# Mixture-of-experts stage: plain fp32 products in 64-token tiles with two column halves, instead of split products in 128-token tiles

## The chip, the cores and the metric

The kernel runs on one core of a Trainium2 chip. The time is the device time of one execution in microseconds; the profile shows one further execution. TensorE (PE) does matrix products, with its weight loads shown apart (PEld), VectorE (DVE), ScalarE (ACT) and GpSimd (POOL) do the rest, and SyncE (SP) issues most of the DMA transfers. Register, branch and semaphore instructions of an engine's sequencer carry a q behind the engine's name (PEldq for TensorE's).

## What is computed

One layer of a decoder trunk for 1024 prompt tokens and 32 sample tokens, in fp32: an adaLN modulation from a conditioning vector, a mixing sub-layer (differential attention beside a short gated convolution), then a channel sub-layer, and a last norm. The change concerns the channel sub-layer, a hierarchical mixture of 32 experts (4 groups of 8); each token goes to the best group and to two experts in it:

```
grp_prob = softmax(t @ w_rg + b_rg);  g_p, g_idx = top_k(grp_prob, 1)
in_grp   = (t @ w_re + b_re) of that group;  e_val, e_idx = top_k(in_grp, 2)
combine  = one_hot(g_idx * 8 + e_idx) weighted with softmax(e_val) * g_p
for e in range(32):
    hid = silu(t @ w_gate[e]) * (t @ w_up[e])          # 1024 -> 256
    out = out + combine[:, e:e+1] * (hid @ w_down[e])  # 256 -> 1024
```

There are 1056 tokens and so 2112 rows of work, and each expert has 3 MB of weights, 96 MB in all.

## The kernel before

Each engine has its own program, written out by hand; semaphores alone order them. In order of time come the modulation (w_ada, three-pass products), the projection to q, k, v (L584, plain fp32), the convolution branch (L612, plain fp32), attention over the prompt (L618 to L676), attention of the samples over the paged cache (L511 to L520 and L679 to L720, with four column groups of 32 addressed at once in L518 and L693), the output projection (three passes), and the expert stage with what plans it.

The plan. VectorE computes the two experts of each token (L1386 to L1414), counts rows per expert with a product (L776 to L778), gives each expert as many tiles of 128 rows as it needs and at least one (L1432 to L1434), sums them up, and writes `plan`: the expert of each tile, the running count of tiles per expert (from `INC`), and `MID`, from which the loops take their number. 18 pairs of selection matrices (L1469 to L1474) and as many products (L783) then give, for each tile and row, the token that is gathered (`xrow`) and the row that is written (`yidx`).

The steps. `expert_steps` (L320) runs the same pattern on every engine: two steps written out, a hardware loop over pairs of tiles, two steps at the end. Step j has buffer b = j % 2:

- TensorE (`expert_products`, L810) looks up the expert of tile j (`expert_of`, a register load from `plan`), finds its weight slot among two by two tests (`in_slot`, L339), and does gate and up at once, 512 columns in 8 chunks. `three_passes` (L526) does each chunk three times in fp32r: leading part by leading part, leading by rest, rest by leading. Then come the 8 transposes of tile j + 1 (L792), the down product of tile j - 1 in 2 chunks and 2 halves of 512 columns, again with a lookup and a search for the slot (`down_products`, L795), and two transposes of `hid` (L826).
- ScalarE (`expert_copies`, L1064) makes the leading part of new weights (L1037 and L1041, only when the expert changes), tanh of the gate (L1069), the leading part of the rows (L1056), the copy of y out of PSUM (L1062) and the leading part of hid (L1081).
- VectorE (`expert_rests`, L1499) makes all rests (L1488, L1492, L1496, L1517) and gated and hid (L1505, L1507).
- GpSimd (`move_rows`, L1649) copies the tile's index column and gathers tile j + 2 from `h2_dram` once tile j has been transposed, then scatters the y of tile j - 1 to `y_dram`.
- SyncE (`load_expert`, L461) loads gate and up of expert e + 1 when expert e - 1 has been multiplied, and down of expert e when down of e - 2 is done: two slots.

Behind the stage each token's two y rows are loaded (L489), weighted, gated, added and normalised.

Of the kernel before, what the change touches and what calls it, by code (L numbers as in the profile page):

```python
# [19 lines left out]
P = 128  # L20
# [14 lines left out]
MAXT = 2 * TOK // P + NE  # L35
# [13 lines left out]
for _name, _w in (("ident", P), ("mask", P), ("upper", P), ("iota", P), ("rope", NT * 96),  # L49
                  ("tokid", 2 * NT), ("valid", NT), ("dmask", LNEW), ("pair", 16), ("sub0", 1), ("sub1", 1),  # L50
                  ("half", 1), ("tilecol", 1)):
    _C[_name] = (_n, _n + _w)
    _n += _w
# [3 lines left out]
def constants():  # L57
# [11 lines left out]
    put("iota", np.broadcast_to(i[None, :], (P, P)).astype(np.float32))  # L69
    pos = np.zeros((NT, P), np.float32)  # L70
# [25 lines left out]
def build(nc, consts, x_prompt, x_sample, cache_k, cache_v, state_conv, page_table, c_prompt, c_sample,  # L96
# [19 lines left out]
    gate_v = w_gate[0].rearrange("e (p c) n -> e p c n", c=DC)  # L116
    up_v = w_up[0].rearrange("e (p c) n -> e p c n", c=DC)
    down_v = w_down[0].rearrange("e (p c) n -> e p c n", c=FC)

    with ExitStack() as ctx:  # L120
# [13 lines left out]
        O_AB, O_X, O_W, O_H, O_VKQ, O_MA = 8 * K, 24 * K, 60 * K, 108 * K, 141 * K, 189 * K  # L134
        cst = at("cst", 0, [P, NCONST])
        small = at("small", NCONST * 4 + 32 - (NCONST * 4) % 32, [P, 224])
        kTs = at("kTs", 6 * K + 960, [P, HEADS, NSAMP])
        qTs = at("qTs", 7 * K + 448, [P, HEADS, NSAMP])
# [83 lines left out]
        hsel = [at(f"hsel{i}", O_MA + 6 * K + 256 * i, [P, TCOLS]) for i in range(4)]  # L222
        xrow = at("xrow", O_MA, [P, TCOLS], I32)
        yidx = at("yidx", O_MA + 256, [P, TCOLS], I32)
# [5 lines left out]
        wgu = [at(f"wgu{i}", O_W + 16 * K * i, [P, 2, DC, FE]) for i in range(2)]  # L230
        wdn = [at(f"wdn{i}", O_W + 32 * K + 8 * K * i, [P, FC, D]) for i in range(2)]
        wguL = [at(f"wguL{i}", O_W + 16 * K * i, [P, 2, DC, FE]) for i in range(2)]
        wdnL = [at(f"wdnL{i}", O_W + 32 * K + 8 * K * i, [P, FC, D]) for i in range(2)]
        wguH = [at(f"wguH{i}", O_VKQ + 16 * K * i, [P, 2, DC, FE]) for i in range(2)]
        wdnH = [at(f"wdnH{i}", O_VKQ + 32 * K + 8 * K * i, [P, FC, D]) for i in range(2)]
        gidx = [at(f"gidx{i}", O_MA + 1024 + 32 * i, [P, 1], I32) for i in range(2)]
        sidx = [at(f"sidx{i}", O_MA + 1088 + 32 * i, [P, 1], I32) for i in range(2)]
        xg = [at(f"xg{i}", O_H + 24 * K + 4 * K * i, [P, D]) for i in range(2)]
        xgH = [at(f"xgH{i}", O_H + 4 * K * i, [P, DC, P]) for i in range(2)]
        xgL = [at(f"xgL{i}", O_H + 8 * K + 4 * K * i, [P, DC, P]) for i in range(2)]  # L240
        th = [at(f"th{i}", O_H + 16 * K + K * i, [P, FE]) for i in range(2)]
        hid = [at(f"hid{i}", O_H + 18 * K + K * i, [P, FE]) for i in range(2)]
        hidH = [at(f"hidH{i}", O_H + 20 * K + K * i, [P, FC, P]) for i in range(2)]
        hidL = [at(f"hidL{i}", O_H + 22 * K + K * i, [P, FC, P]) for i in range(2)]
        gated = [at(f"gated{i}", O_MA + 2 * K + K * i, [P, FE]) for i in range(2)]
        yrow = [at("yrow0", O_MA + 4 * K, [P, D]), at("yrow1", O_MA + 12 * K, [P, D])]
# [31 lines left out]
        ones = at("ones", O_H + 15 * K, [P, P])  # L278
        slot_i = at("slot_i", O_H + 14 * K + 256, [P, 2 * NT], I32)
# [13 lines left out]
        wgate_in0 wgate_in1 wup_in0 wup_in1 wdn_in0 wdn_in1 wguH_done wguL_done wdnH_done wdnL_done gidx_done sidx_done xg_in0 xg_in1 go_on  # L293
        xgT_ps xgH_done xgL_done gu_ps th_done hid_done hidT_ps hidH_done hidL_done y_ps y_done y_out0 y_out1
# [1402 lines left out]
```

## Time and profile before

| | |
|---|---|
| median of 3 runs | 1499.11 us (1498.01 to 1502.76) |
| the profiled execution | 1495.69 us, span 1493.8 us |
| TensorE products | 1235.5 us busy, 83% of the span |
| weight loads of TensorE | 846.9 us, 57% |
| VectorE | 745.9 us, 50% |
| ScalarE | 569.4 us, 38% |
| GpSimd | 264.0 us, 18% |
| HBM | 170 GB/s over the span |

Busy time is that of the engine's own instructions; products overlap their predecessors, so a busy TensorE is not one at its peak. The expert stage runs from about 984 us, the first gather, to about 1433 us, the last store of rows.

### The profile page before, as it was taken

Reading aid. Unit: us, or ns where it says so; the run is one execution under the profiler, and the core shown is the slowest. Engines: PE = TensorE matmul, PEld = TensorE weight load, DVE = VectorE, ACT = ScalarE, POOL = GpSimd, SP = SyncE. Lnnn points to the kernel's source line nnn. Section 1 sums busy time; section 2 is a strip of 40 time slices with the busy share of each in tenths; the row PEclk is TensorE's granted clock in tenths of the full one; section 3 lists DMA queues with packets and bytes.
Section 4 is the critical chain, followed back from the end, with each engine's and each line's share of the span. In section 5 each row is a group of like instructions: output and inputs, shape, how many; then the busy total and the mean of one; then the engine's idle time right before and its main releaser. Section 6 shows DMA issues by size and latency. Waiting matters only on the chain.

```text
span 1493.8 us, 20962 instructions
## 1 busy us (share of the span) xinstructions
PE 1235.5 (83%) x6201; PEld 846.9 (57%) x6202; DVE 745.9 (50%) x1101; ACT 569.4 (38%) x786; POOL 264.0 (18%) x289
## 2 busy tenths in 40 slices
PE   4879999999999689965787999458899999989920
PEld 1334444456666456644566787247777777777710
DVE  4772232101110787721113454658855656888747
ACT  4541110000000455542334222117744646777623
POOL 0020100010000111000000011013524334544323
PEclk9989999999999899986866999659999999999965
DMA  8991200011100200037777211408856667887545
GB/s 282 375 328 46 88 21 22 29 47 43 43 0 0 86 0 1 0 104 249 228 225 249 82 43 43 176 26 318 314 223 243 244 235 270 314 325 299 207 171 181
DMA packets 84547, 230.91 MB, mean 155 GB/s; under 512 B 16101, under 2 KB 28517, under 8 KB 72165
## 3 DMA queue, kind: packets, MB, share of 16 engines
q1 hardware_dynamic: 70288, 203.80, 38.5%
q0 software_dynamic: 14192, 26.24, 4.9%
q8 instruction: 39, 0.64, 0.2%
q14 instruction: 28, 0.23, 0.0%
HBM read 220.42 MB, written 34.21 MB: 170 GB/s over the span
## 4 chain that ended last, share of the span: by engine, by line
PE 57%; DVE 12%; issue 8%; SPq 7%; DMA 6%; ACT 5%; DVEq 2%; POOL 1%; ACTq 1%; POOLq 0%
PE psum L531 22%; PE psum L584 12%; PE psum L612 11%; SPq L407 3%; DMA xg<-h_scratch,gidx 2%; PE psum L630 2%; DVE xgL L1496 2%; DMA wada<-in_w_ada_dram 2%; DVEq L333 2%; PE psum L639 2%; SPq L416 1%; ACT pexp L925 1%; SPq L423 1%; PE psum L673 1%; PE psum L738 1%
## 5 line engine op out<-in xcount | busy, mean ns | idle before, releaser
L584 PE MATMUL psum<-wqkv,hT 128*128 128x512 f32 (+1 forms) x432 | 187.6, 594 | 0.0
L612 PE MATMUL psum<-hT,wcv 128*128 128x352 f32 x576 | 170.9, 459 | 0.0
L1488 DVE TENSOR_TENSOR wguL<-wgu,wguH 128x2048 fp32r<-128x2048 f32 x64 | 146.8, 2294 | 41.1 <-ACT wguH L1037 40.4
L531 PE MATMUL psum<-wguH,xgH 128*128 128x512 f32 x320 | 130.8, 409 | 32.8 <-DVE xgL L1496 32.8
L612 PEld LDWEIGHTS psum<-hT,wcv 128*128 128x128 f32 x576 | 109.3, 190 | 60.6
L584 PEld LDWEIGHTS psum<-wqkv,hT 128*128 128x128 f32 (+1 forms) x432 | 77.9, 182 | 103.2 <-issue 103.2
L1037 ACT CAST wguH<-wgu 128x2048 fp32r<-128x2048 f32 x64 | 120.2, 1910 | 20.4 <-issue 13.9
L531 PE MATMUL psum<-wguH,xgL 128*128 128x512 f32 x320 | 126.7, 396 | 0.0
L531 PE MATMUL psum<-wguL,xgH 128*128 128x512 f32 x320 | 126.4, 395 | 0.0
L1556 POOL TENSOR_SCALAR small<-small 128x1 f32<-128x1 f32 (+3 forms) x36 | 19.8, 551 | 467.5 <-ACT ajunk L1014 169.5
L630 PE MATMUL psum<-kT,qz 128*128 128x512 f32 (+3 forms) x192 | 77.7, 520 | 19.5 <-ACT pexp L925 18.2
L531 PEld LDWEIGHTS psum<-wguH,xgH 128*128 128x128 f32 x320 | 61.2, 191 | 50.2 <-issue 38.6
L1492 DVE TENSOR_TENSOR wdnL<-wdn,wdnH 128x2048 fp32r<-128x2048 f32 x32 | 73.2, 2288 | 14.8 <-ACT wdnH L1041 14.6
L1209 DVE TENSOR_TENSOR cuT<-psum,cg_sb 128x352 f32<-128x352 f32 (+1 forms) x12 | 6.2, 514 | 133.6 <-ACT cg_sb L911 133.5
L531 PE MATMUL psum<-wdnH,hidH 128*128 128x512 f32 x160 | 67.1, 420 | 5.1 <-issue 3.1
L1643 POOL COPY sidx<-yidx 128x1 int32 (+1 forms) x40 | 39.0, 975 | 182.4 <-ACT yrow L1062 182.3
L1041 ACT CAST wdnH<-wdn 128x2048 fp32r<-128x2048 f32 x32 | 61.0, 1906 | 26.3 <-issue 26.3
L531 PEld LDWEIGHTS psum<-wguH,xgL 128*128 128x128 f32 x320 | 61.1, 191 | 13.5
L531 PEld LDWEIGHTS psum<-wguL,xgH 128*128 128x128 f32 x320 | 61.3, 192 | 11.7
L911 ACT COPY cg_sb<-psum 128x352 f32<-128x352 f32 x12 | 5.4, 452 | 162.2 <-PE psum L612 162.2
L708 PE MATMUL psum<-cst,kseq 128*128 128x128 f32 x256 | 48.4, 327 | 22.6 <-DMA kseq<-in_cache_k_dram 21.9
L969 ACT COPY kTp<-psum 128x512 f32<-128x512 f32 x64 | 37.3, 586 | 76.6 <-PE psum L708 76.5
(269 smaller groups left out, 2320.7 us busy)
## 6 DMA issues: line engine op xcount, KB each, us to landing
wgu<-in_w_gate_dram SPq DMA_DIRECT2D x32, 1024.0 KB, 5.0
wgu<-in_w_up_dram SPq DMA_DIRECT2D x32, 1024.0 KB, 7.5
wdn<-in_w_down_dram SPq DMA_DIRECT2D x32, 1024.0 KB, 7.1
wada<-in_w_ada_dram SPq DMA_DIRECT2D x24, 1024.0 KB, 8.3
kseq<-in_cache_k_dram SPq DMA_DIRECT2D x64, 256.0 KB, 3.0
vseq<-in_cache_v_dram SPq DMA_DIRECT2D x64, 256.0 KB
yg<-y_scratch SPq DMA_DIRECT2D x16, 512.0 KB, 5.4
wqkv<-in_w_in_dram SPq DMA_DIRECT2D x1, 6144.0 KB, 24.9
```

The source lines that it names most:

```text
L407: return sp.value_load(pt_sb[0:1, s * PAGES + p:s * PAGES + p + 1], min_val=0, max_val=kc.shape[0] - 1)
L531: ins = mm(out, r32(x(c)), r32(w(c)), start=(begin and c == 0 and k == 0), stop=(end and c == chunks - 1 and k == 2))
L584: last = mm(psum[0:n, 2 + j, :], hT[:, c, P * t:P * t + n], wqkv[:, c, AW * j:AW * j + AW], start=(c == 0), stop=(c == DC - 1))
L612: last = mm(psum[:, 3 * (n % 2) + j, 0:TB], wcv[i % 2][:, c, j, :], hT[:, c, TB * tb:TB * tb + TB], start=(c == 0), stop=(c == DC - 1))
L630: last = mm(psum[:, 2 * u + a // 512, 0:b - a], qz[i % 2][:, u, h, :], kT[:, h, a:b], start=True, stop=True)
L708: last = tr(psum[:, 4 + n % 2, P * c:P * c + P], kseq[half % 3][:, p % 4, P * c:P * c + P], ident)
L969: nc.scalar.copy(kTp[n % 2][:, :, :], psum[:, 4 + n % 2, :].rearrange("p (c n) -> p c n", c=4)).then_inc(S["kp_sb"], 1)
L1037: nc.scalar.copy(r32(wguH[slot][:, g, :, :]), wgu[slot][:, g, :, :]).then_inc(S["wguH_done"], 1)
L1041: nc.scalar.copy(r32(wdnH[slot][:, :, :]), wdn[slot][:, :, :]).then_inc(S["wdnH_done"], 1)
L1488: TT(r32(wguL[slot][:, g, :, :]), wgu[slot][:, g, :, :], wguH[slot][:, g, :, :], ALU.subtract).then_inc(S["wguL_done"], 1)
L1492: TT(r32(wdnL[slot][:, :, :]), wdn[slot][:, :, :], wdnH[slot][:, :, :], ALU.subtract).then_inc(S["wdnL_done"], 1)
L1643: nc.gpsimd.tensor_copy(sidx[b][:, :], yidx[:, bass.ds(j, 1)]).then_inc(S["sidx_done"], 1)
```

## The change

Expert tiles hold 64 tokens. The row of a token is taken as two half rows of 512: a tile has 128 partitions, of which the first 64 hold the first halves of 64 tokens and the other 64 the second halves. Four transposes instead of eight turn them into `xT`, in which a chunk of 128 features has 64 token columns. All products are plain fp32 calls. Each chunk's 64 token columns are the stationary side of two calls that write PSUM partitions 0 to 63 and 64 to 127: for gate and up these are the two halves of the 256 hidden columns (128 of gate and 128 of up each), for down the two halves of the 1024 output columns. So gated, hid and y have 128 partitions and half the columns. The splits, their tiles and their semaphores are gone. Four slots hold whole experts; three experts are loaded as soon as the residual is done, the fourth once the router's inputs are free. The index columns are copied by VectorE instead of GpSimd. Four steps instead of two are written out ahead of the loop. The plan counts tiles of 64 by an addition and a shift instead of eight comparisons. The diff, cut to its core:

```diff
-MAXT = 2 * TOK // P + NE
+TW = 64
+NSLOT = 4
+MAXT = 2 * TOK // TW + NE
...
-    gate_v = w_gate[0].rearrange("e (p c) n -> e p c n", c=DC)
-    down_v = w_down[0].rearrange("e (p c) n -> e p c n", c=FC)
+    gate_v = w_gate[0].rearrange("e (h p k) n -> e p h k n", h=2, k=4)
+    down_v = w_down[0].rearrange("e (c p) n -> e p c n", c=FC)
+    h2_halves = h2_dram.rearrange("t (h c) -> (t h) c", h=2)
+    y_halves = y_dram.rearrange("r (h c) -> (r h) c", h=2)
...
+        LEAD = 4
         def expert_steps(eng, step, mid):
-            for b in range(2):
-                step(b, b, 0, True, 2)
+            for j in range(LEAD):
+                step(j, j % 2, j // 2, 2)
             with eng.Fori(0, mid) as m:
                 for b in range(2):
-                    step(2 * m + (2 + b), b, m + 1, False, 2)
+                    step(2 * m + (LEAD + b), b, m + LEAD // 2, 2)
...
-        def in_slot(eng, e, body, new=1):
-            for slot in range(2):
-                bit = (e + (1 - slot)) & 1
-                with eng.If(((bit + new) >> 1) > 0):
+        def in_slot(eng, e, body):
+            for slot in range(NSLOT):
+                with eng.If(((e + (NSLOT - slot)) & (NSLOT - 1)) < 1):
                     body(slot)
...   SyncE
             sp.wait_ge(W["x1_done"], 2 * NT)
-            load_gate_up(0, 0)
+            for e in range(3):
+                load_gate_up(e, e)
+                load_down(e, e)
...
+            sp.wait_ge(W["rexp_in"], 2)
+            sp.wait_ge(W["lg_ps"], NT)
+            load_gate_up(3, 3)
+            load_down(3, 3)
...
+            with sp.Fori(0, NE // NSLOT - 1) as m:
+                for slot in range(NSLOT):
+                    e = NSLOT * m + (NSLOT + slot)
+                    before = sp.value_load(plan[0:1, bass.ds(e + (INC - NSLOT), 1)], min_val=1, max_val=MAXT)
+                    sp.wait_ge(W["gu_ps"], before)
+                    load_gate_up(e, slot)
+                    sp.wait_ge(W["y_ps"], before)
+                    load_down(e, slot)
...   TensorE
             def gather_transposes(b):
-                for c in range(DC):
-                    last = tr(psum[:, c // 4, P * (c % 4):P * (c % 4) + P], xg[b][:, c:D:DC], ident)
+                for k in range(4):
+                    last = tr(psum[:, b, P * k:P * k + P], xg[b][:, k:512:4], ident)
...   down_products
-                    pe.wait_ge(W["hidL_done"], j + 1)
-                    pe.wait_ge(W["wdnL_done"], e + 1)
-                    for n in range(2):
-                        a = slice(512 * n, 512 * n + 512)
-                        last = three_passes(psum[:, 5 + n, :], lambda c: hidH[b][:, c, :], lambda c: hidL[b][:, c, :],
-                                            lambda c: wdnH[slot][:, c, a], lambda c: wdnL[slot][:, c, a], FC)
+                    pe.wait_ge(W["hidT_sb"], j + 1)
+                    pe.wait_ge(W[f"wdn_in{slot}"], 16 * (e >> 2) + 16)
+                    for c in range(FC):
+                        for n in range(2):
+                            last = mm(psum[TW * n:TW * n + TW, 5 + b, :], hidT[b][:, TW * c:TW * c + TW], wdn[slot][:, c, 512 * n:512 * n + 512],
+                                      start=(c == 0), stop=(c == FC - 1))
...   expert_products
-                    pe.wait_ge(W["xgL_done"], j + 1)
-                    pe.wait_ge(W["wguL_done"], 2 * e + 2)
-                    three_passes(...).then_inc(S["gu_ps"], 1)
+                    pe.wait_ge(W["xT_sb"], j + 1)
+                    pe.wait_ge(W[f"wgu_in{slot}"], 32 * (e >> 2) + 32)
+                    for c in range(DC):
+                        h, k = divmod(c, 4)
+                        for n in range(2):
+                            last = mm(psum[TW * n:TW * n + TW, 2 + b, 0:FE].rearrange("p (g f) -> p g f", g=2), xT[b][:, k, TW * h:TW * h + TW],
+                                      wgu[slot][:, :, h, k, P * n:P * n + P], start=(c == 0), stop=(c == DC - 1))
+                    last.then_inc(S["gu_ps"], 1)
...   VectorE, one step (expert_rests before)
+            def expert_rows(j, b, i, left):
                 dve.wait_ge(W["th_done"], j + 1)
+                STT(gated[b][:, :], th[b][:, :], 1.0, psum[:, 2 + b, 0:P], ALU.add, ALU.mult).then_inc(S["m_dve_step"], 1)
                 dve.wait_ge(S["m_dve_step"], j + 1)
+                STT(hid[b][:, :], gated[b][:, :], 0.5, psum[:, 2 + b, P:2 * P], ALU.mult, ALU.mult).then_inc(S["hid_done"], 1)
+                if left == 2:
+                    dve.wait_ge(W["xgT_ps"], j + 1)
+                    gather_index(j + 2, b)
+                if past(j, 1):
+                    scatter_index(j - 1, 1 - b, i - 1 + b)
+                dve.wait_ge(W["hidT_ps"], j + 1)
+                nc.vector.tensor_copy(hidT[b][:, :], psum[:, 4, 0:P]).then_inc(S["hidT_sb"], 1)
...   GpSimd, one step
                 if left == 2:
-                    pool.wait_ge(W["xgT_ps"], j + 1)
-                    pool.sem_inc(S["go_on"], 1)
                     gather_rows(j + 2, b)
-                if not (first and b == 0):
+                if past(j, 1):
                     scatter_rows(j - 1, 1 - b)
```

`past(j, n)` is true in the loop and for written-out steps from n on. In a step ScalarE keeps tanh (128 columns), the copy of the transposed rows (512) and the copy of y (512). `expert_rests` and `expert_copies` lose the rest.

## Rows read from the trace of the kernel before

**Rows 1.** Page, part 4: the chain that ended last, share of the span by line.
```profile
PE psum L531 22%; PE psum L584 12%; PE psum L612 11%; SPq L407 3%; DMA xg<-h_scratch,gidx 2%; PE psum L630 2%; DVE xgL L1496 2%; DMA wada<-in_w_ada_dram 2%; DVEq L333 2%; PE psum L639 2%; SPq L416 1%; ACT pexp L925 1%; SPq L423 1%; PE psum L673 1%; PE psum L738 1%
```

**Rows 2.** Windows: stretch, its length, engines' busy us (instructions), clock, DMA share, GB/s.
```profile
997.20:1101.60 104.40, 91.58 (x405) 74.52 (x406) 80.09 (x62) 72.53 (x62) 38.23 (x31) 0.94 0.75 286
1101.60:1250.50 148.90, 138.44 (x656) 114.21 (x655) 82.92 (x80) 78.24 (x79) 55.89 (x60) 0.99 0.59 223
1250.50:1418.00 167.50, 153.16 (x735) 126.75 (x734) 139.35 (x109) 126.09 (x109) 74.98 (x60) 1.00 0.77 293
```

**Rows 3.** Line L1069: duration ns min/median/max, first and last start.
```profile
L1069 ACT ACTIVATE th<-psum x40: 370/385/385, 1005.8 to 1421.4; 128x256 f32<-128x256 f32 x40
```

**Rows 4.** Chain of waits of one step: start us, us, what.
```profile
1247.42 5.75 PE psum L531 x24
...
1253.61 0.43 DVE gated L1505
...
1256.68 1.23 DVE xgL L1496
```

**Rows 5.** Timeline, TensorE, plain fp32: start us, us, instruction, count.
```profile
326.89 15.36 PE L612 MATMUL psum<-hT,wcv 128*128 128x352 f32 x51
...
667.21 0.43 PE L518 MATMUL psum<-kTp,qbd 128*32 128x128 f32 x8
...
722.42 3.64 PE L693 MATMUL psum<-vseq,aTs 128*32 128x128 f32 x64 [0.54 <-DVE aTs L1308]
```

**Rows 6.** Chain of waits near 1412: transposes, then a down product.
```profile
1411.97 0.88 PE psum L792 x8
1412.85 2.77 PE psum L531 x12
```

**Rows 7.** TensorE's sequencer: a read and tests, 1243.9:1245.3; 1255.7:1256.8; all tests.
```profile
L333 PEldq FUSED_REGOPS  x2: 43/100/157, 1244.0 to 1244.5; - x2
...
L343 PEldq ALU_OP  x2: 32/34/36, 1244.8 to 1244.8; - x2
...
L813 PEldq ALU_OP  x1: 36/36/36, 1245.2 to 1245.2; - x1
...
L343 PEldq ALU_OP  x3: 36/36/36, 1255.7 to 1256.3; - x3
...
L343 PEldq COMPARE_BRANCH  x160: 67/154/357, 993.9 to 1424.2; - x160
```

**Rows 8.** TensorE's sequencer: two waits that it reached, by line.
```profile
L609 PEldq EVENT_SEMAPHORE  x1: 51/51/51, 335.9 to 335.9; - x1
...
L706 PEldq EVENT_SEMAPHORE  x1: 51/51/51, 725.0 to 725.0; - x1
```

**Rows 9.** A full gather; landings of L1637 in 1262:1400, 1120:1165 and 990:1010.
```profile
1250.41 3.01 POOL L1637 DMA_INDIRECT xg<-h_scratch,gidx  x1 [0.86 <-POOL gidx L1634]
...
DMA to landing us min/median/max: 7.7/8.2/8.9
...
DMA to landing us min/median/max: 5.2/7.9/10.5
...
DMA to landing us min/median/max: 3.0/4.6/9.2
```

**Rows 10.** DMA queues, 1262:1400: packets, MB, share of 16 engines.
```profile
q1 hardware_dynamic: 5643, 41.07, 76.4%
q0 software_dynamic: 3744, 2.67, 6.0%
```

**Rows 11.** DMA queue of code, 1000:1400: blocks, MB, share.
```profile
q8 instruction: 2, 0.03, 0.0%
```

**Rows 12.** First transposes; end of the stage (timeline, then chain of waits).
```profile
992.75 1.97 PE L792 MATMUL psum<-cst,xg 128*128 128x128 f32 x8 [11.02 <-DMA xg<-h_scratch,gidx]
...
1429.06 1.02 ACT yrow L1062
...
1433.90 4.77 DMA yg<-y_scratch
```

More of the change, by code:

```diff
@@ L227, in build @@
         vmap = at("vmap", O_MA + 8 * K, [P, 3, TCOLS])
[L230 to L235, printed above, removed]
+        SLOT = (O_W, O_W + 24 * K, O_VKQ, O_VKQ + 24 * K)
+        wgu = [at(f"wgu{i}", SLOT[i], [P, 2, 2, 4, FE]) for i in range(NSLOT)]
+        wdn = [at(f"wdn{i}", SLOT[i] + 16 * K, [P, FC, D]) for i in range(NSLOT)]
         gidx = [at(f"gidx{i}", O_MA + 1024 + 32 * i, [P, 1], I32) for i in range(2)]
         sidx = [at(f"sidx{i}", O_MA + 1088 + 32 * i, [P, 1], I32) for i in range(2)]
[L238 to L246, printed above, removed]
+        xg = [at(f"xg{i}", O_H + (16 + 2 * i) * K, [P, 512]) for i in range(2)]
+        xT = [at(f"xT{i}", O_H + (20 + 2 * i) * K, [P, 4, P]) for i in range(2)]
+        yrow = [at(f"yrow{i}", O_H + (24 + 2 * i) * K, [P, 512]) for i in range(2)]
+        th = [at(f"th{i}", O_H + 28 * K + 512 * i, [P, P]) for i in range(2)]
+        gated = [at(f"gated{i}", O_H + 29 * K + 512 * i, [P, P]) for i in range(2)]
+        hid = [at(f"hid{i}", O_H + 30 * K + 512 * i, [P, P]) for i in range(2)]
+        hidT = [at(f"hidT{i}", O_H + 31 * K + 512 * i, [P, P]) for i in range(2)]
         gate_fp = at("gate_fp", O_AB, [P, D]); gate_fs = at("gate_fs", O_AB + 4 * K, [P, D])
@@ L1078, in expert_copies @@
-                if not (first and b == 0):
-                    copy_y(j - 1, 1 - b, i - 1 + b, not first)
-                act.wait_ge(W["hidT_ps"], j + 1)
-                nc.scalar.copy(r32(hidH[b][:, :, :]), psum[:, 4, 0:FE].rearrange("p (c n) -> p c n", c=FC)).then_inc(S["hidH_done"], 1)
+                    copy_rows(1 - b)
+                if past(j, 1):
+                    copy_y(j - 1, 1 - b, i - 1 + b)
             act.wait_ge(W["xgT_ps"], 1)
-            lead_rows(0)
+            copy_rows(0)
@@ L1479, in _ @@
             link(TT(vmap[:, 1, :], vmap[:, 1, :], vmap[:, 0, :], ALU.add))
+            for k in range(2):
+                link(TS(vmap[:, k, :], vmap[:, k, :], 2.0, C("side"), ALU.mult, ALU.add))
             link(nc.vector.tensor_copy(xrow[:, :], vmap[:, 1, :]))
             nc.vector.tensor_copy(yidx[:, :], vmap[:, 0, :]).then_inc(S["plan_done"], 1)
-            mid = dve.value_load(plan[0:1, MID:MID + 1], min_val=NE // 2 - 2, max_val=MAXT // 2 - 2)
-            def rest_gate_up(e, slot, g):
-                dve.wait_ge(W["wguH_done"], 2 * e + (g + 1))
-                TT(r32(wguL[slot][:, g, :, :]), wgu[slot][:, g, :, :], wguH[slot][:, g, :, :], ALU.subtract).then_inc(S["wguL_done"], 1)
@@ L1511, in expert_rests @@
-                if first and b == 0:
-                    rest_down(0, 0)
-                else:
-                    e = expert_of(dve, j)
-                    in_slot(dve, e, lambda slot: rest_down(e, slot), step_of(e, expert_of(dve, j - 1)))
-                dve.wait_ge(W["hidH_done"], j + 1)
-                TT(r32(hidL[b][:, :, :]), psum[:, 4, 0:FE].rearrange("p (c n) -> p c n", c=FC), hidH[b][:, :, :],
-                   ALU.subtract).then_inc(S["hidL_done"], 1)
-            for g in range(2):
-                rest_gate_up(0, 0, g)
```

177 lines of the change are left out of this document (70 added, 107 removed).

## The prediction

> **What bounds the kernel now.** I read the chain of waits first. A fifth of the span is TensorE in L531, the three-pass product, and most of that lies in the expert stage, the only stage that this change rewrites [rows 1]. The table by stretch says that this stage is not TensorE alone: over its three thirds the engine counts 92, 138 and 153 us of 104, 149 and 168, the clock is nearly always the full 2.4 GHz, and the DMA engines move 223 to 293 GB/s [rows 2]. So neither is full. The gate/up product of the first tile ends at 1005.8 (where its tanh starts) and that of the fortieth at 1421.4 [rows 3]: 39 steps of 10.66 us, 415.6 us. The chain of one step tells what a step is: 5.75 us of products, then gated and hid, then VectorE's remainders of weights and rows up to the end of xgL at 1257.9, and only then the next product [rows 4]. The split's remainders on VectorE hold each step, not the products.
>
> **The change part by part.**
>
> *Number of steps.* The reference's routing on its own inputs gives, per expert, 67 65 7 28 28 50 9 10 | 87 286 176 142 110 120 229 354 | 27 11 12 17 34 48 48 7 4 28 6 16 52 5 20 9 rows. In tiles of 128, with at least one each, that is 39, padded to 40; in tiles of 64 it is 53, padded to 54. So 39 steps become 53. Twenty-two of the 53 are experts with one tile.
>
> *What goes.* All splits and remainders (wguH, wguL, wdnH, wdnL, xgH, xgL, hidH, hidL): the chain of rows 4 loses its VectorE part, and ScalarE and VectorE keep half-width work of some 2 us a step each. What is late next has to be found among the array, TensorE's sequencer, the gathers and the loads.
>
> *The array.* A plain fp32 call runs as two events with two weight loads (288 calls of L612 are 576 events). In the convolution 51 of them take 15.36 us, of which the last one lasts 0.46: 0.298 us for 352 columns, 0.847 ns a column [rows 5]. Do two column halves run at once? In L518, where four groups of 32 columns are addressed, 8 events fit into 0.43 us though each lasts about 0.27, and in L693 64 start in 3.2 us, 0.051 each, where one event of 128 columns alone needs 0.108 at the full clock [rows 5]. They do. Gate/up is then 8 chunks x 2 x 256 columns = 3.47 us, down 2 x 2 x 512 = 1.73, four transposes half of today's 0.88 [rows 6], the hid transpose 0.11: 5.75 us; with up to 0.4 for four changes between tiled and whole array, 5.75 to 6.2. Today's is 5.75 + 0.88 + 2.77 + 0.23 [rows 4, 6].
>
> *TensorE's sequencer.* This is the term that I think decides. Each step looks for its slot twice (gate/up and down), now among four slots instead of two, and every test costs whether taken or not. Reading the expert number takes from 1244.0 to 1244.8, 0.76; a test that is entered from there to L813 at 1245.2, 0.45; one that is skipped 1255.7 to 1256.3, 0.6 [rows 7]. The new test has one register operation less (no shift), 0.12 by the spacing of the operations: 0.33 and 0.48. Two searches are 2 x (0.76 + 3 x 0.48 + 0.33) = 5.05 us; counters, waits with a register value and the loop 0.85 more (8 operations of about 0.1). Now 3.3 of this is hidden behind 10.66 us. Does it hide still? The sequencer runs ahead of the array by a bounded count: at 335.9 it reached the wait behind the second group of L612, which had begun at 326.9; 30 of 48 events had started, so 18 events and their loads, 36 instructions, were outstanding. At 725.0, in the tiled L693, some 22 events, 43 instructions [rows 5, 8]. I take 38. Gate/up is 64 instructions, at 0.054 us each; so 26 must be through before the sequencer leaves it: 1.4 us. Issuing the other 26 instructions 0.3. Sum: 5.05 + 0.85 + 1.4 + 0.3 = 7.6 us a step, above the array's 6.2. If the shift stays in the test, 8.6; if most of the search hides, the array's 6.2.
>
> *Gathers.* A gather's index is now copied on VectorE behind hid, so gather j+2 starts about 2.2 us after gate/up j ended (tanh, gated, hid at half width, the index, and the 0.86 in front of the DMA [rows 9]), and it has to be there before the transposes behind gate/up j+1. From those transposes to the end of the next gate/up are about 6.0 us. So two steps need 2.2 + L + 6.0, L being issue to landing. L is 8.2 us in the median while weights load, 7.9 where tiles are mixed, and 3.0 at the least; a full gather keeps POOL 3.0 us instead of 1.0 [rows 9]. With L = 8.2 a step is 8.2 us, with 4.5 it is 6.4. Today the weights' packets are 8 KB and the rows 4 KB; both halve, so I expect a shorter L; the gathers stay at or just under 7.6 and I add 0.3 for those that don't: **7.9 us a step**, the value nearest to both rows.
>
> *Weight loads.* In the single-tile stretch the weight queue holds the 16 engines 76.4% and the gathers and scatters 6.0% of steps of 10.6 us [rows 10]: 8.1 + 0.64 = 8.75 us of transfer an expert. Experts 16 to 31 are sixteen such steps, but three slots are full when expert 15 ends: 13 loads of 8.75 = 114 us against 15 steps of 7.9 = 118. Just hidden. If steps were 6.2 this would bind there, for some 20 us.
>
> *Ends.* The first transposes started at 992.75 at the half clock [rows 12]; four instead of eight, half a copy, no xgL, and 2 x 3.47 at the half clock put the first gate/up's end at 1001.4 instead of 1005.8; with the index copied on VectorE, -5 us. Behind the last gate/up lie 12.1 us until the rows are stored, before yg is loaded at 1433.9; without hidH, hidL and with half the copy of 1.02 [rows 12] about 10: -2. The plan drops eight 0.2 us comparisons for four operations and gains three: nothing. The 9 MB loaded ahead run while the plan is made; nothing on the path waits for that queue but the stores of h2, 0 to 2 us, within the range.
>
> **Sum**, against the profiled execution's own 1495.7 us (span 1493.8 and 1.9 around it): 1495.7 - 5 - 2 - 415.6 + 53 x 7.9 = 1491.8. The median shown is 3.4 above that execution, so 1495, against 1499.1. Each of 39 steps becomes 2.8 us shorter, 108 us, and 14 new ones of 7.9 come in, 111. Even is 8.0 us a step.
>
> **The rivals.**
>
> *A step is the array's (6.4 us).* For it: were the sequencer free to run further ahead, the 1.4 us of stall and much of the search would vanish behind the products. Against: rows 8. Time: 1073.1 + 53 x 6.4 = 1412, 1416 in the median. The Trainium skill (Advanced Engine Details and Errata, Engine Queue Depths) gives TensorE 64 places "complicated with tiling", which would let the whole of gate/up in at once. The trace shows 36 and 43.
>
> *The gathers set the step: the side on which it is slower.* Place: the transposes waiting for xg. It decides from L = 7.8 us on. With 8.4 for the 22 single tiles (8.3 a step) and 9.8 for the 31 full ones (9.0; their POOL time is the 3.0 us of rows 9, and loads of 3 MB run into them) it is 1073.1 + 183 + 279 = 1535, 1538 in the median. For it: today's 7.7 to 8.9 in a loaded queue. Against: the packets halve.
>
> *Code is fetched anew.* TensorE's loop grows from about 390 to about 780 instructions; today no more than 2 blocks of code came in 400 us [rows 11]. Were it three blocks per two steps at some 2 us each, a step would be 10.9 and the kernel 1654. The Trainium skill (Runtime: NRT & Kernel Launch, Instruction fetch mechanics) says that a taken branch out of the loaded window waits for a DMA of code, and gives TensorE room for 2048 instructions. By that figure the loop fits; no row of this trace shows that size.
>
> *The halves do not run side by side* (64 wide groups are not in this trace, 32 wide ones are): 5.2 us more in the array, 11.2 a step, 1670.
>
> **How the numbers follow.** Forecast with steps of 7.5 to 8.4, 1474 to 1522 around 1495: 0.58. Array's step 0.15, gathers 0.14, code 0.07, halves one after the other 0.06. Within 0.3% (about what a measurement of this kernel can tell from no change) means steps between 7.9 and 8.05: 0.11, all of it in the forecast, which gives 0.27 to faster and 0.20 to slower. With the rivals: faster 0.42, same 0.11, slower 0.47. The range, 1425 to 1555, holds the forecast, the gathers' case and more than half of the array's; it leaves out 0.13 for the last two and 0.06.
>
> **What would show it.** Steps from tanh to tanh of 7.5 to 8.4 us, 54 of them, with the register operations of L343 busy nearly throughout; L531 gone from the stage; pairs of fp32 events starting together; waits before the gate/up product put down to issue, not to xT or the weights. Wrong: steps at 6.2 to 6.5 (the search hides), waits on xg longer than 1 us in most steps, tanh waiting 10 us or more, a code queue that runs all through the stage, or weights late before the last expert.

## The result and the profile after

The changed kernel takes 1519.0 us in the median of four runs (1511.8 to 1521.2), the kernel before took 1499.0 us beside it: ratio 1.0128, interval 1.0101 to 1.0155. The forecast was 1495 us, no difference; it is 1.3% slower, inside the stated range, on the side that the forecast gave 0.47. The profiled execution has a span of 1517.9 us against 1493.8, and all of the 24.1 us is in the expert stage.

The tanh behind the gate/up products (line 1059 of the changed kernel), which answers to [rows 3]; columns: duration min/median/max, first and last start:

```profile
L1059 ACT ACTIVATE th<-psum x54: 277/277/278, 1001.7 to 1448.6; 128x128 f32<-128x128 f32 x54
```

There are 54 of them, so the tile count was right. Forty tiles took 415.6 us from first to last; 54 take 446.9, or **8.43 us for each of 53 steps**, where 7.9 was forecast and 8.0 was even. The start came 4.1 us earlier (1001.7 for 1005.8), the part behind the last tanh is 3.1 us shorter (69.3 us of span for 72.4). Together: -4.1 - 3.1 - 415.6 + 446.9 = +24.1.

The same stage by windows, answering to [rows 2] (stretch, length, busy us with instructions of TensorE products, weight loads, VectorE, ScalarE, GpSimd, then clock, DMA share, GB/s):

```profile
1001.72:1448.55 446.83, 357.98 (x2377) 185.91 (x2377) 56.84 (x263) 76.13 (x158) 105.89 (x104) 0.97 0.64 236
987.00:1100.00 113.00, 86.52 (x536) 44.35 (x536) 12.90 (x63) 17.12 (x36) 24.59 (x24) 0.88 0.69 253
1100.00:1300.00 200.00, 159.46 (x1086) 83.97 (x1088) 26.13 (x121) 34.99 (x73) 49.21 (x49) 0.99 0.46 163
1300.00:1455.00 155.00, 123.96 (x812) 63.25 (x808) 19.30 (x89) 26.05 (x54) 35.26 (x35) 0.96 0.75 286
```

VectorE and ScalarE have little left to do (57 and 76 us of 447). TensorE's products fill 358 of 447 us, so 89 us are idle. The clock is lower in the first and last stretch, where the DMA share is higher, than in the middle one; the first stretch also begins at the half clock.

Two pieces of the chain of waits show the two kinds of step. A quiet one, from 1101.37 to 1109.87 (start us, us, what):

```profile
1101.37 3.67 PE psum L822 x32
...
1105.07 0.75 PE psum L796 x4
1105.82 0.69 issue
1106.51 1.94 PE psum L808 x8
1108.44 0.26 PE psum L833
1108.70 1.17 issue
1109.87 3.67 PE psum L822 x32
```

Nothing is late here but TensorE's own sequencer: "issue" stands ahead of the down products (L808) and of the next gate/up (L822). The same trace shows how far the sequencer runs ahead, the 1.4 us in the prediction's sum. It reaches the wait in front of this gate/up (L818) at 1101.2 and the first instruction behind it, a test of the next search (L346), at 1102.7; TensorE's timeline up to 1102.73 stands below them:

```profile
L818 PEldq FUSED_REGOPS  x1: 75/75/75, 1101.2 to 1101.2; - x1
L346 PEldq ALU_OP  x1: 32/32/32, 1102.7 to 1102.7; - x1
1101.37 1.73 PE L822 MATMUL psum<-wgu,xT 128*64 128x256 f32 x14 [1.56 <-issue]
```

When it leaves the gate/up, 14 of its 32 events have started: 18 events with their weight loads, 36 instructions, are still out. For about 1.4 us in every step it can't search.

Now a step with a late gather, behind the tanh at 1370.94, and below it the window 1378 to 1390 (columns as above):

```profile
1372.80 5.82 DMA xg<-h_scratch,gidx
...
1378.66 0.75 PE psum L796 x4
1379.41 1.92 issue
1381.33 3.68 PE psum L808 x8
1385.01 0.41 PE psum L833
1385.42 4.30 PE psum L822 x32
...
1378.00:1390.00 12.00, 9.42 (x48) 4.38 (x49) 0.86 (x5) 1.40 (x3) 2.03 (x2) 0.72 0.91 351
```

The rows land at 1378.62. The down search, which follows the wait for them in TensorE's order, could not start before: 1.92 us of issue. Then the down products take 3.68 where the quiet step has 1.94, and the gate/up 4.30 for 3.67, at the lower clock level after the idle time: the granted clock was 0.72 from 1378 to 1390 and 1.00 in the 12 us before. The next gate/up ends at 1389.72, 11.1 us behind the landing. This is one of the dearest cases. In 13 steps the products of the transposes waited for rows; from the start of these transposes to the next tanh they took 8.2 to 11.4 us, 9.5 in the mean. Slow products are not in all of them: 6 of the 53 down products took over 3 us.

TensorE's waits between the first and the last tanh (engine, line, waited for: us, times, longest), and below them the test instructions, the landings of all 54 gathers, and the DMA queue of code in 1050 to 1440 (blocks, MB, share):

```profile
PE psum L822 <- issue: 47.5, 40, 2.1
PE psum L808 <- issue: 28.9, 27, 2.1
PEld psum L796 <- DMA xg<-h_scratch,gidx: 18.6, 18, 2.1
PE psum L796 <- DMA xg<-h_scratch,gidx: 10.5, 13, 1.6
```

```profile
L346 PEldq COMPARE_BRANCH  x424: 77/208/437, 1003.6 to 1448.5; - x142
...
DMA to landing us min/median/max: 2.1/4.9/7.2
...
q8 instruction: 1, 0.02, 0.0%
```

The 424 comparisons are 8 for each of 53 steps. Eighteen weight loads of transposes waited for rows, and in 13 of these cases the products too. By stretch the landing's median is 3.4 us in 1100 to 1300 and 5.8 in 1300 to 1440.

### The profile page after: what moved, and what is told of

It is laid out like the page before. It is cut to its first block, busy times and chain, and to the rows that moved or that the text cites. A ratio compares the mean times of both kernels' runs of the same rounds, so it can differ in the third digit from the quotient of the medians.

```text
span 1517.9 us, 20398 instructions
## 1 busy us (share of the span) xinstructions
PE 1211.3 (80%) x6791; PEld 714.2 (47%) x6792; DVE 493.1 (32%) x1112; ACT 362.6 (24%) x691; POOL 193.1 (13%) x237
## 4 chain that ended last, share of the span: by engine, by line
PE 60%; issue 10%; DMA 9%; DVE 8%; SPq 8%; ACT 3%; POOL 1%; POOLq 0%; DVEq 0%; ACTq 0%
PE psum L588 12%; PE psum L616 11%; PE psum L822 10%; PE psum L535 9%; PE psum L808 6%; DMA xg<-h_scratch,gidx 6%; SPq L410 3%; PE psum L634 2%; DMA wada<-in_w_ada_dram 2%; PE psum L796 2%; SPq L426 2%; PE psum L643 2%; SPq L419 1%; ACT pexp L931 1%; PE psum L677 1%
## 5 line engine op out<-in xcount | busy, mean ns | idle before, releaser
L822 PE MATMUL psum<-wgu,xT 128*64 128x256 f32 x1728 | 204.6, 391 | 49.1 <-issue 47.5
L822 PEld LDWEIGHTS psum<-wgu,xT 128*64 128x64 f32 x1728 | 125.3, 140 | 114.0 <-issue 63.4
L808 PE MATMUL psum<-wdn,hidT 128*64 128x512 f32 x432 | 114.1, 652 | 31.0 <-issue 29.3
L1611 POOL DMA_INDIRECT xg<-h_scratch,gidx x54 | 55.2, 1022 | 259.4 <-DVE gidx L1475 254.6
L1619 POOL DMA_INDIRECT y_scratch<-yrow,sidx x54 | 54.9, 1016 | 136.8 <-ACT yrow L1055 125.3
L535 PE MATMUL psum<-woutH,mixH 128*128 128x512 f32 (+1 forms) x144 | 58.6, 407 | 5.8 <-DVE mixL L1318 5.8
L808 PEld LDWEIGHTS psum<-wdn,hidT 128*64 128x64 f32 x432 | 28.2, 142 | 74.2 <-issue 72.4
L1116 DVE TENSOR_TENSOR wadaL<-wada,wadaH 128x2048 fp32r<-128x2048 f32 x24 | 54.3, 2287 | 19.3 <-ACT wadaH L883 19.3
L535 PE MATMUL psum<-wadaH,condTH 128*9 128x512 f32 x96 | 39.7, 414 | 23.2 <-DVE wadaL L1116 23.1
L535 PE MATMUL psum<-woutL,mixH 128*128 128x512 f32 (+1 forms) x144 | 57.8, 401 | 0.0
L535 PE MATMUL psum<-woutH,mixL 128*128 128x512 f32 (+1 forms) x144 | 57.5, 400 | 0.0
```

What stands on the lines that cost most here:

```text
L535: ins = mm(out, r32(x(c)), r32(w(c)), start=(begin and c == 0 and k == 0), stop=(end and c == chunks - 1 and k == 2))
L808: last = mm(psum[TW * n:TW * n + TW, 5 + b, :], hidT[b][:, TW * c:TW * c + TW], wdn[slot][:, c, 512 * n:512 * n + 512], start=(c == 0), st ...
L822: last = mm(psum[TW * n:TW * n + TW, 2 + b, 0:FE].rearrange("p (g f) -> p g f", g=2), xT[b][:, k, TW * h:TW * h + TW], wgu[slot][:, :, h, ...
L1116: TT(r32(wadaL[n % 6][:, :, :]), wada[n % 6][:, :, :], wadaH[n % 3][:, :, :], ALU.subtract).then_inc(S["rest_done"], 1)
L1611: nc.gpsimd.indirect_dma_start(xg[b][:, :], None, h2_halves, bass.IndirectOffsetOnAxis(ap=gidx[b][:, 0:1], axis=0), bounds_check=2 * TOK - ...
L1619: nc.gpsimd.indirect_dma_start(y_halves, bass.IndirectOffsetOnAxis(ap=sidx[b][:, 0:1], axis=0), yrow[b][:, :], None, bounds_check=4 * TOK ...
```

## The experiments

All times are medians beside runs of the kernel before; "step" is the tanh's last start less its first over 53 (over 39 for tiles of 128) in the profiled execution, which can lie off the median: that of e3 took 1499.4 us, the longest of its ten.

| kernel | step us | median us | ratio to before (95%) |
|---|---|---|---|
| the changed kernel | 8.43 | 1519.0 | 1.0128 (1.0101-1.0155) |
| e1 index early | 7.64 | 1476.3 | 0.9852 (0.9811-0.9892) |
| e2 two more tests | 9.60 | 1584.8 | 1.0569 (1.0524-1.0614) |
| e3 two-test search | 8.09 | 1493.1 | 0.9949 (0.9927-0.9971) |
| e4 = e1 + e3 | 6.97 | 1435.7 | 0.9568 (0.9532-0.9603) |
| e5 = e4, two slots | 7.73 | 1481.3 | 0.9869 (0.9823-0.9916) |
| e6 = e1, register reused | 7.52 | 1469.6 | 0.9776 (0.9726-0.9825) |
| e7 before, no splits | 11.40 | 1522.4 | 1.0134 (1.0087-1.0181) |
| e8 = e4 + e6 | 7.02 | 1438.9 | 0.9586 (0.9541-0.9631) |
| e9 = e4, transposes twice | 7.08 | 1444.3 | 0.9657 (0.9625-0.9689) |
| e10 = e1, transposes twice | 7.89 | 1489.7 | 0.9937 (0.9916-0.9958) |
| e11 down products first | 8.05 | 1495.7 | 0.9989 (0.9971-1.0007) |
| e12 = e3 + e11 | 7.22 | 1453.4 | 0.9705 (0.9672-0.9738) |

### e1: the gathers a little earlier

```diff
 def expert_rows(j, b, i, left):
+    if left == 2:
+        dve.wait_ge(W["xgT_ps"], j + 1)
+        gather_index(j + 2, b)
     dve.wait_ge(W["th_done"], j + 1)
     ...
-    if left == 2:
-        dve.wait_ge(W["xgT_ps"], j + 1)
-        gather_index(j + 2, b)
```

> The index copy that releases the gather of tile j + 2 stands at the head of step j on VectorE, ahead of its wait for the tanh. My theory (TensorE's slot search sets the quiet step at 7.84 us, the other 0.59 us per step are late gathers and the products at half clock behind them): the gather is issued about 3 us earlier, waits of the transposes on a gather nearly vanish, steps come to 7.8 to 7.95 us, so 25 to 33 us less than the changed kernel: 1487 to 1494 us. Rival one, the landings are long because of the weight traffic and late by more than 3 us: less than 12 us gained. Rival two, the half clock comes from TensorE's idle time while it searches and not from gathers: half-clock products stay, and under 10 us are gained.

Moving one 0.15 us copy gained 43 us, more than my theory had (25 to 33). The stage of e1, same columns as above:

```profile
997.14:1401.87 404.73, 342.71 (x2377) 182.88 (x2377) 55.73 (x262) 76.14 (x159) 104.93 (x103) 1.00 0.69 260
```

Its waits for the expert stage hold no line for xg at all, and issue stays (L822: 44.0 us in 40 waits). The 42.1 us that the stage lost divide into busy time, 358.0 - 342.7 = 15.3 us that was products at the half clock, and idle time, 88.9 - 62.0 = 26.8 us. The idle time can be split further by TensorE's waits in e1's stage (the changed kernel's lines stand above):

```profile
PE psum L822 <- issue: 44.0, 40, 2.0
PE psum L808 <- issue: 13.4, 15, 1.5
```

Issue ahead of the down products fell from 28.9 to 13.4 us and ahead of gate/up from 47.5 to 44.0, the 10.5 us of products waiting for rows are gone, and 2.8 us of waiting for weights ahead of gate/up, in two waits, are new: 26.7 us. So about 18 late gathers cost 42 us, 2.3 us each, and only a quarter of it is the lateness: 19 us are search that stands behind it and is no longer hidden, 15 us products at the half clock. Against the second rival: TensorE still idles 15% of the stage in e1 and the granted clock is 1.00, so the gaps of the search as they are in e1 don't lower it. Longer ones do, as e2 shows.

### e2: more of the search

```diff
 def in_slot(eng, e, body):
     ...
+    for n in range(2):
+        with eng.If(((e + (8 + n)) & 63) < 1):
+            eng.wait_ge(W["plan_done"], 1)
```

> Two more tests that are never true stand in each of TensorE's two searches. The instructions of a skipped test took 0.47 to 0.48 us. If the search sets the step, each step gains 4 x 0.48 = 1.9 us, over 53 steps 101 us, less up to 31 us because the gathers then have more time: 1589 to 1620 us. If the gathers or the array set it, the tests lie beside other work and under 25 us are added (below 1544 us).

The median lies 4 us below the expected interval, because that was reckoned with 31 us for the late gathers and e1 shows 42. Against e1, where they are gone, a step is 9.60 - 7.64 = 1.96 us longer for four tests of 0.48, 1.92. With longer steps the gathers are nearly in time here as well (their weight loads wait 1.3 us in all). The agreement is closer than it deserves, because the longer search brings the half clock with it, without a late gather. The stage of e2 in the columns of the windows, and pieces of TensorE's timeline:

```profile
1001.70:1510.40 508.70, 386.77 (x2377) 200.64 (x2377) 56.98 (x263) 76.31 (x159) 106.04 (x104) 0.92 0.56 207
...
1395.70 2.64 PE L811 MATMUL psum<-wdn,hidT 128*64 128x512 f32 x8 [1.94 <-issue]
...
1409.25 5.36 PE L825 MATMUL psum<-wgu,xT 128*64 128x256 f32 x32 [1.98 <-issue]
```

The products are busy 44 us longer than in e1 (386.8 for 342.7), at a clock of 0.92: of the 1.96 us a step 0.83 are longer products and 1.13 idle time. How much of the longer products lay beside search that was needed anyway was not separated. The side is clear: what TensorE waits for is issue, and the sequencer sets the step. It can be seen directly in e1, too. Between 1190 and 1230 its register, branch and semaphore instructions leave no gap above 0.2 us but one of 1.42 us per step, the one between L818 and the first instruction behind gate/up. In e4 (below) a second gap of 0.9 to 1.1 us per step appears between 1180 and 1200: there it has time to spare.

### e3 and e4: a shorter search

```diff
-    for slot in range(NSLOT):
-        with eng.If(((e + (NSLOT - slot)) & (NSLOT - 1)) < 1):
-            body(slot)
+    with eng.If((e & 2) < 1):
+        with eng.If((e & 1) < 1):
+            body(0)
+        with eng.Else():
+            body(1)
+    with eng.Else():
+        ...                   # body(2), body(3) likewise
```

> TensorE finds its slot by two tests (bit 1 of the expert's number, then bit 0) with an else, in place of four tests in a row. If each of the two tests costs 0.25 to 0.45 us, a search is 0.9 to 1.2 us shorter, a step 1.8 to 2.4 us. Search theory: the sequencer needs 5.4 to 6.0 us per step, and what is late next is the gather (issued 1.9 us behind the tanh, needed at the next gate and up products' end) or the array's own 6.2: steps of 6.3 to 7.4 us, 1406 to 1465 us. If the gathers already set the step of the changed kernel: 1510 us or more.

> Both: the two-test search and the early index copy. If search and gather are the two things that stand above the array, the step comes to 6.2 to 6.6 us: 1400 to 1424 us, and it is at least 15 us below the kernel with the two-test search alone. If the array alone sets the step once the search is short, the two are within 8 us of each other.

Neither hit its interval. e3 alone gains only 26 us: its quiet steps are 6.4 and 6.7 us, but every second one or so is 10 to 12. A piece of its chain of waits:

```profile
1097.18 7.00 DMA xg<-h_scratch,gidx
...
1104.22 0.75 PE psum L803 x4
1104.97 0.85 issue
1105.82 3.62 PE psum L815 x8
...
1109.70 3.60 PE psum L829 x32
```

A gather of 7.0 us again, 0.85 us of the shorter search behind it, down products at the half clock, and the next gate/up ends at 1113.30, 9.1 us behind the landing. A quicker step makes the gathers later: 33.1 us of waiting for xg in 19 transposes against 10.5 in 13. With both edits, e4, it is 1435.7 us, **4.3% faster than the kernel before** and 83 us below the changed one, the best of this study. The edits are worth 43 and 26 us alone and 83 together. TensorE in e4 (timeline; start, us, line, instruction, count):

```profile
1186.76 3.67 PE L829 MATMUL psum<-wgu,xT 128*64 128x256 f32 x32 [0.25 <-issue]
1190.37 0.75 PE L803 MATMUL psum<-cst,xg 128*128 128x128 f32 x4
1191.05 1.94 PE L815 MATMUL psum<-wdn,hidT 128*64 128x512 f32 x8
1192.92 0.33 PE L840 MATMUL psum<-cst,hid 128*128 128x128 f32 x1
1193.17 3.67 PE L829 MATMUL psum<-wgu,xT 128*64 128x256 f32 x32
```

From start to start 6.41 us with no gap in the step shown: the array's step. Ahead of about every second gate/up some 0.25 us of issue are left, as in the first row (steps of 6.4 and 6.7 us take turns), so the search is not quite off the path. e4 misses its 1400 to 1424 by the weights at the end. The seven steps before the last one take 8.5, 8.4, 10.3, 6.8, 10.2, 6.6 and 10.0 us, 15 us above 6.54 each; an early step with a late gather takes 10.8. The chain at the end is

```profile
1338.80 19.70 DMA wgu<-in_w_up_dram
```

### e5: two slots

e4 with `NSLOT = 2`, `e >> 1` in the two waits for weights, and one test with an else.

> Early index copy and a search by tests with an else, but two weight slots in place of four (one test, and experts are loaded one to two ahead). If the depth of the loads is worth nothing: 1428 to 1438 us, as with four slots or a little less. My theory is that it is worth something, because the kernel with four slots already waits for gate and up weights in its last steps (10.0 to 10.8 us for a step where the quiet one has 6.4): with two slots each of the 22 steps with an expert of its own waits for some 3.1 MB at about 400 GB/s (7.8 us, 10 with the issue and what shares the queues), up to 3.5 us each: 1455 to 1515 us.

It costs 45 us by the ratios, inside the interval. The middle steps stay at 6.4 to 6.5, where e4 has 6.4 and 6.7 in turn: with one test per search no issue stands ahead of gate/up any more. The steps of single tiles alternate between 6.5 and 12 to 14.8, with waits for wgu in the chain:

```profile
1321.90 10.07 DMA wgu<-in_w_up_dram
1332.01 5.36 PE psum L821 x32
```

The gate/up behind the wait takes 5.36 us for 3.67, and the stage's granted clock is 0.94, with no wait for a gather in it.

### e6 and e8: one load of the expert number less in every second step

```diff
-    down_products(j - 1, 1 - b)
+    down_products(j - 1, 1 - b, held[0] if b else None)   # e as step b == 0 left it in the register
```

> The kernel with the early index copy, and in every second step TensorE takes the expert's number of the down search from the register of the step before and does not load it again. A load took 0.76 us of the sequencer, so half the steps get 0.76 us shorter if the sequencer sets the step: 53 x 0.38 = 20 us below the kernel with the early index alone (1476 us): 1452 to 1460 us. If the array or the gathers set its steps of 7.64 us: 1472 us or more.

> The reused register on top of the two-test search and the early index copy. The array is busy 347 of the 369 us of that kernel's expert stage, so the sequencer should no longer decide: 1429 to 1441 us, no difference that can be measured. If the sequencer still sets every second step (the idle 0.25 us ahead of some gate and up products), up to 7 us less; if it still sets all of them, 20 us less (1416 us).

e8 is as expected: nothing. e6 missed; it gained 7 to 11 us (medians, ratios), hardly more than the scatter of the two kernels' intervals, and 0.12 us a step where 0.38 was expected, although the edit saves more than I had counted. With the number in a register from the step before, its tests need no new register operations; between 1233.2 and 1234.7 the sequencer's test line shows only

```profile
L346 PEldq COMPARE_BRANCH  x4: 70/202/219, 1233.6 to 1234.6; - x4
```

Three skipped tests at about 0.26 us and one entered: some 0.9 us of search for 2.5. In TensorE's timeline of e6 the wait shifts instead of going: ahead of the gate/up products at 1208.77, 1216.46, 1223.84, 1231.85, 1239.69 stand 0.92, 0.69, 0.90, 1.15 and 1.36 us of issue, in both kinds of step. The sequencer's own rows show where it goes. Its last instruction ahead of the hid transpose (L837) and the loop's first one behind it (L329):

```profile
L837 PEldq ALU_OP  x1: 36/36/36, 1219.6 to 1219.6; - x1
L329 PEldq ALU_OP  x1: 32/32/32, 1221.1 to 1221.1; - x1
```

Between them it stands still for 1.5 us, and so in every second step between 1200 and 1260, behind the shortened search (1.43 to 1.67 us); between 1190 and 1230 e1 has no such gap. A sequencer that is done early in one step is held there and cannot bring that time into the next step, where the full searches stand. What holds it, I read as the limit of its run-ahead; no run changes that limit. Cutting both searches of every step (e4 against e1: 0.67 us a step, down to the array) worked.

### e7: one part alone, the splits taken out of the kernel before

Its three passes become one plain fp32 product on the loaded weights; ScalarE's leads and VectorE's rests of weights, rows and hidden values go; tiles of 128, whole rows and two slots stay.

> One part of the change alone: the kernel before with the splits taken out of the experts (one plain fp32 product in place of three passes, no lead and rest of weights, rows and hidden values), with its tiles of 128 tokens, its whole rows and its two slots. From the halves' times (32 calls of 64 wide in 3.67 us, 8 of the down products in 1.87) full 128-token tiles need 2 x 3.61 + 2 x 1.87 + the transposes of 8 and 2 blocks 2 x 0.94 us less some start: 12.0 to 12.9 us per step against 10.66 before, over 39 steps 52 to 87 us more than before: 1550 to 1590 us. If VectorE or ScalarE with the splits had set the step of the kernel before, its removal gains and the time is below 1500 us.

It is 1.3% slower than before and 28 us under the interval: 11.40 us a step for the 12.0 to 12.9 that I took. Its chain of waits is nothing but products:

```profile
1199.81 3.44 PE psum L804 x8
1203.24 0.23 PE psum L829 x2
1203.47 6.87 PE psum L817 x16
1210.34 0.89 PE psum L792 x8
```

3.44 + 0.23 + 6.87 + 0.89 = 11.43 us. I had doubled the halves' times, and whole tiles take less than that (6.87 us for 2 x 3.60, 3.44 for 2 x 1.87). Without the smaller tiles the plain product loses; it is the 64-wide halves side by side (6.87 and 3.44 us become 3.60 and 1.87) that pay for 14 more tiles. The change as made (1.0128) ends where e7 does (1.0134): what the smaller tiles win, the search and the gathers take.

### e9 and e10: more work for the array alone

```diff
-for k in range(4):
+for k in 2 * list(range(4)):
     last = tr(psum[:, b, P * k:P * k + P], xg[b][:, k:512:4], ident)
```

> On the kernel with the two-test search and the early index copy, TensorE transposes the gathered rows twice into the same place: four more products of 0.17 us, 0.68 us of the array per step. If the array sets the step there, 53 x 0.68 = 36 us are added to its 1436 us: 1464 to 1476 us, less up to 6 us of the idle 0.25 us ahead of some gate and up products. If the sequencer still sets it, the products lie beside the search and under 12 us are added.

> The same four transposes more on the kernel with the early index copy and four tests per search (1476 us, step 7.64 us, array busy 343 of 405 us). If TensorE's sequencer sets its step, the added 0.68 us fills idle array time and only the eight more instructions are issued: 0 to 12 us more, 1474 to 1488 us. If the array's time adds to the step whatever the search does (search and products in a row, not side by side), 36 us more: 1505 us or above.

The dose was smaller than I wrote: eight events take 1.17 us in the chain where four take 0.68, so 0.49 us a step, 26 us in all. e9 added 13 us by the ratios and 9 by the medians: not the 28 to 40 us of the array theory, but about the 12 us at most of the other. e10 also added 13 (expected up to 12). TensorE in e9:

```profile
1187.07 3.67 PE L829 MATMUL psum<-wgu,xT 128*64 128x256 f32 x32
1190.68 1.23 PE L803 MATMUL psum<-cst,xg 128*128 128x128 f32 x8
...
1193.97 3.67 PE L829 MATMUL psum<-wgu,xT 128*64 128x256 f32 x32
```

Every quiet step is 6.90 us with no idle time: the array sets it. In e4 steps of 6.4 and 6.7 take turns, so about 0.36 us was added to a quiet step, and the rest of the stage gave much of it back: the last steps wait for weights anyway, and the late gather of e4's step of 10.8 us is not there. In e10 a step of 7.64 became 7.89, half of the dose. A quarter of these 13 us is one early step of 11.8 us, which has no late gather: 2.87 us of issue, then a gate/up of 5.36 us at the half clock. By the total the two cannot be told apart; by the timelines they can: no gap in e9, 0.9 and 1.4 us of issue ahead of gate/up in e10.

### e11 and e12: what stands behind the wait

```diff
-if left:
-    pe.wait_ge(W[f"xg_in{1 - b}"], 16 * (i + 1 + b))
-    gather_transposes(1 - b)
 if past(j, 1):
     down_products(j - 1, 1 - b)
+if left:
+    pe.wait_ge(W[f"xg_in{1 - b}"], 16 * (i + 1 + b))
+    gather_transposes(1 - b)
```

and ScalarE copies y ahead of the rows.

> The changed kernel with the gathers where they are, but TensorE does the down search and its products ahead of the wait for the gathered rows and their transposes. Theory: a late gather costs so much (42 us for 18 to 19 late ones, 2.3 us each) because the down search stands behind the wait in TensorE's order and is then not hidden; what is lost is its lateness, some 1.9 us of search and products at the half clock. With the order turned round, a gather may land 3 us later and nothing but the transposes stands behind it: steps of 7.6 to 7.9 us, 1476 to 1495 us. Rival, only the landing counts and what stands behind it does not: the waits move with the transposes and under 10 us are gained (1509 us or more).

> The same order with the two-test search, gathers not earlier. In the two-test kernel late gathers set every second step (8.09 us a step in the mean, 6.4 for a quiet one, 1493 us). Theory: with 3 us more room most gathers are in time, but the copy of the transposed rows (0.6 us and its start) is now in front of the next gate and up products: 7.0 to 7.5 us a step, 1436 to 1463 us. Rival: 1483 us or more.

e11 gained 21 us by the ratios and 23 by the medians; at 1495.7 us it lies 0.7 above its interval, and its mean step of 8.05 us above the 7.6 to 7.9 of the theory. e12 is in its interval. TensorE's waits in e11:

```profile
PE psum L822 <- ACT xT L1049: 41.8, 46, 1.5
...
PEld psum L796 <- DMA xg<-h_scratch,gidx: 1.6, 2, 0.8
```

The waits for xg fell from 18.6 to 1.6 us, with the gathers issued where they were. In their place the gate/up products wait for the copy of the rows, which now has only one small transpose to hide behind: its quiet steps are 7.9 to 8.0 us, not 7.7. The clock in its stage is 0.99 and the products' busy time 340.9 us, about that of e1 (342.7). The order gives a gather more time and takes the search from behind it at once, so e11 does not price the two apart; the waits of e1 do.

## Why the forecast was off

- *Tiles, array, halves.* Right. 53 steps; 32 gate/up events in 3.67 us (3.47 forecast), 8 down events in 1.94 (1.73), array's step 6.41 in e4 (5.75 to 6.2 forecast, a little low). The 64-wide halves do run side by side; that rival (1670) is out.
- *The sequencer.* Right: 7.64 us a step once nothing else is late (e1), forecast 7.6; a skipped test 0.49 us (e2), forecast 0.48; 36 instructions out and 1.4 us of stall, forecast 38 and 1.4. That the mean comes within 0.04 us is luck in part: e1's steps behind the first lie between 6.4 and 8.5 us, the 0.85 and the 0.3 us were not measured by themselves, and e2's test price has the half clock in it. The rival that most of it hides (1416) is out. The Trainium skill gives TensorE 64 places in its queue (Advanced Engine Details and Errata, Engine Queue Depths); were the whole gate/up let in at once, nearly all of the search would have hidden behind it. The measurement decides against that reading here: 36 were out when the sequencer left gate/up, and issue stood ahead of the gate/up products for 47.5 us of the changed kernel's stage.
- *Gathers.* **This is the step that failed**: "from those transposes to the end of the next gate/up are about 6.0 us", and hence "the gathers stay at or just under 7.6 and I add 0.3". The landing did become shorter (4.9 us in the median of the stage; before, it was 8.2, as in [rows 9]). But 6.0 us is about the array's own sum, and the search that the paragraph before it had priced is left out. With every gather in time that stretch is 7.7 us in the mean (e1), behind a late one 9.5 (changed kernel) or 9.1 (e3): the down search stands behind the wait and then hides behind nothing, and some products run at the half clock. And a gather issued 1.9 us behind the tanh is late from 7.64 - 1.9 = 5.7 us of landing on, about the median of the last stretch (5.8). The 0.3 us was 0.79 (8.43 - 7.64), 42 us instead of 16; these 26 us are nearly all of the 28 by which the profiled execution missed its sum (1519.8 for 1491.8). I treated the two limits as a maximum, 7.6 or the gathers' pair of steps; they add up where one engine does both in order. e1 removed the cause and got 43 us; e11 took the search from behind the wait, and the waits for rows fell from 18.6 to 1.6 us for 23 us of time.
- *The rival of slower gathers* had the right side and the right place, the wrong price: it set steps by landings of 8.4 and 9.8 us, which did not come (7.2 at the most). Its "decides from L = 7.8 us on" is where a step reaches the even 8.0; by its own formula the gathers set the step from L = 7.0 on.
- *Code.* Inside the loop one block of code came in 390 us; the rival (1654) is out. The Trainium skill (Runtime: NRT & Kernel Launch, Instruction fetch mechanics) gives TensorE room for 2048 instructions, and with a loop of some 780 this trace agrees. On the way into the loop (1003 to 1050) 7 blocks came on the same queue. Steps there are long in e10 (11.8 us) and e11 (12.8 us) with nothing but issue to wait for; whether code is the cause stays open.
- *What bound the kernel before* was read too far: "The split's remainders on VectorE hold each step, not the products". TensorE's own work was 5.75 + 0.88 + 2.77 + 0.23 = 9.6 of the 10.66 us, and the page puts 32.8 us of waiting in 40 tiles on xgL. The forecast used the measured 10.66 and doesn't hang on it.
- *Weights.* Right: hidden in the changed kernel and nearly in e1, and with short steps they bind at the end, 15 us in e4 where 20 were forecast. Two slots cost 45 us at that speed.
- *Ends.* -4.1 for -5 and -3.1 for -2.
- *The range* was said to hold more than half of the array's case, whose own time, 1416, lies below its 1425; the share was not worked out.

## What to carry to other kernels

Two limits on one in-order engine are not a maximum: whatever stands behind a wait is no longer hidden once that wait is late, so look at the order behind it and price the late case with it, half clock included. Register reads and tests count as work of their engine: in a step of 7.6 us the slot search of four tests was the bound, and two tests with an else plus one index copy moved forward turned 1.3% slower into 4.3% faster. Remove both limits before judging either: 43 and 26 us alone, 83 together.

## What the runs showed of the hardware

- Plain fp32 products with 64 stationary columns, sent in turn to the two halves, take about half the time of as many streamed columns at 128: 3.60 us for 6.87 (32 events of 256 columns in e3, 16 of 512 in e7), 1.87 for 3.44.
- TensorE's sequencer had 36 instructions out, 18 fp32 events with their weight loads, when it left a gate/up of 64 (changed kernel).
- The half clock came behind long gaps, whatever made them. In e1 the granted clock was 1.00 over the whole stage with TensorE idle for 15% of it in short pieces. In the changed kernel, with late gathers, it was 0.97, and products behind them took up to twice as long (3.68 us for 1.94), 15.3 us in all. With a longer search and hardly a late gather (e2) it was 0.92, with waits for weights alone (e5) 0.94.
- A test of an expression that is already in a register costs its branch alone, 0.26 us for 0.48 (e6).
